# Two modulation blocks before the recurrence's first products, and 13 filler steps per pass in place of 14

## The reference, cut to what matters

```python
def step(S, inp):
    r_t, w_t, k_t, v_t, kk_t, a_t = inp
    sa = jnp.einsum('dbhvk,dbhk->dbhv', S, kk_t)
    S = (S * w_t[..., None, :] - sa[..., :, None] * (kk_t * a_t)[..., None, :]
         + v_t[..., :, None] * k_t[..., None, :])
    return S, jnp.einsum('dbhvk,dbhk->dbhv', S, r_t)
...
bonus = jnp.sum(jnp.sum(r * k * r_k, axis=-1, keepdims=True) * v, axis=0).reshape(B, L, C)
```

```python
s_lat = jax.nn.silu(c)[:, None, :]
s_ctx = jax.nn.silu(c_ctx)
for l in range(DEPTH):
    ml = jnp.split(s_lat @ w_mod[l] + b_mod[l], N_MOD, axis=-1)
    mc = jnp.split(s_ctx @ w_mod[l] + b_mod[l], N_MOD, axis=-1)
```

## Time and profile before

| | us |
|---|---|
| median of 3 runs | 3142.22 |
| lowest and highest of them | 3133.02, 3143.27 |
| the profiled execution | 3134.65 |
| its span (first to last instruction) | 3133.4 |
| PE busy in the span | 3004.9 |
| the four passes of the recurrence (first products of pass 0 to the last carried products) | 193.8 to 413.5 |

### The profile page before, as it was taken

How to read it: one execution, slowest core, us unless ns; L and a number is a source line. 1 busy time by engine, 2 the same in 40 slices (tenths; PEclk the granted TensorE clock), 3 DMA queues, 4 the chain that set the end, 5 groups by cost and what they waited for, 6 DMA issues and landing times.

```text
span 3133.4 us, 43817 instructions
## 1 busy us (share of the span) xinstructions
PE 3004.9 (96%) x18486; PEld 2429.1 (78%) x18486; DVE 1374.3 (44%) x2855; ACT 582.4 (19%) x1339; POOL 37.3 (1%) x60
## 2 busy tenths in 40 slices
PE   8988999999899999999999899999999999999999
PEld 7656778898488978888854447888878888765999
DVE  3264533433523544445222625445244453225675
ACT  1232222113412021100021621010010100124110
POOL 0000000002000000000000000000000000000000
PEclk9999999999999999999999999999999999999999
DMA  6667854366244452222212102222422222331453
GB/s 235 219 227 258 288 173 154 107 190 175 81 131 134 129 175 70 92 64 74 91 56 77 54 28 81 81 75 62 118 83 81 82 73 74 108 90 43 149 150 107
DMA packets 355846, 371.06 MB, mean 118 GB/s; under 512 B 7395, under 2 KB 282228, under 8 KB 355524
## 3 DMA queue, kind: packets, MB, share of 16 engines
q1 hardware_dynamic: 351828, 361.18, 36.5%
q0 software_dynamic: 2208, 5.31, 0.9%
q10 hardware_dynamic: 1616, 1.77, 0.2%
HBM read 367.19 MB, written 1.05 MB: 118 GB/s over the span
## 4 chain that ended last, share of the span: by engine, by line
PE 90%; DVE 5%; ACT 3%; issue 2%; DMA 0%; DVEq 0%; ACTq 0%
PE acc L132 74%; PE aux L132 15%; ACT sb_xn L275 1%; PE aux L2191 1%; DVE sb_work L1924 0%; DVE sb_work L1921 0%; ACT sb_work L1723 0%; ACT sb_work L1725 0%; DVE sb_xn L253 0%; ACT sb_rstd L266 0%; DVE sb_work L1935 0%; ACT sb_rstd L268 0%; DVE sb_work L1703 0%; DMA sb_x<-xT 0%; DVE sb_work L2341 0%
## 5 line engine op out<-in xcount | busy, mean ns | idle before, releaser
L132 PE MATMUL acc<-sb_xn,weights 128*128 128x256 f32 (+2 forms) x5184 | 1211.4, 388 | 16.2 <-DVE sb_xn L253 10.3
L132 PEld LDWEIGHTS acc<-sb_xn,weights 128*128 128x128 f32 x5184 | 942.2, 190 | 239.6 <-issue 118.8
L132 PE MATMUL acc<-sb_work 128*128 128x256 f32 (+1 forms) x1944 | 374.6, 346 | 0.0
L132 PEld LDWEIGHTS acc<-sb_work 128*128 128x128 f32 x1944 | 323.8, 191 | 34.7 <-issue 0.4
L132 PE MATMUL acc<-sb_work,weights 128*128 128x256 f32 (+2 forms) x1508 | 322.4, 361 | 3.2 <-DVE sb_work L1238 1.4
L132 PE MATMUL acc<-sb_big,weights 128*128 128x256 f32 (+1 forms) x1776 | 315.2, 334 | 4.1 <-issue 3.9
L132 PEld LDWEIGHTS acc<-sb_big,weights 128*128 128x128 f32 x1776 | 279.3, 192 | 30.8 <-issue 5.3
L132 PEld LDWEIGHTS acc<-sb_work,weights 128*128 128x128 f32 x1508 | 254.2, 191 | 54.3 <-issue 26.1
L1453 DVE TENSOR_TENSOR sb_work<-weights 128x512 f32<-128x512 f32 (+1 forms) x112 | 99.7, 890 | 160.6 <-PE acc L132 160.6
L1425 ACT COPY sb_work<-acc 128x256 f32<-128x256 f32 (+1 forms) x112 | 38.0, 339 | 704.7 <-PE acc L132 704.7
L132 PE MATMUL aux<-sb_xn,sb_work 128*128 128x256 f32 (+1 forms) x704 | 151.3, 359 | 8.9 <-ACT sb_xn L275 8.9
(11 more groups left out here) (305 smaller groups left out, 2591.8 us busy)
## 6 DMA issues: line engine op xcount, KB each, us to landing
weights<-ffn_w_up SPq DMA_DIRECT2D x88, 1024.0 KB, 7.9
weights<-w_mod SPq DMA_DIRECT2D x36, 2048.0 KB, 8.5
weights<-ffn_w_down SPq DMA_DIRECT2D x48, 1408.0 KB, 7.1
weights<-ffn_w_gate SPq DMA_DIRECT2D x44, 1024.0 KB, 5.4
weights<-w_in SPq DMA_DIRECT2D x8, 2048.0 KB, 8.0
weights<-mix_w_in SPq DMA_DIRECT2D x6, 2048.0 KB, 12.3
weights<-na_w_qkv SPq DMA_DIRECT2D x6, 2048.0 KB, 10.1
weights<-ple_w_gate SPq DMA_DIRECT2D x4, 2048.0 KB, 8.3
```

The lines of the kernel that those rows point to most:

```text
L132: return te.matmul(o, lhsT, rhs, start=start, stop=stop, skip_group_check=True)
```

## The change

The constant 20 takes the place of 16 as the base of `fill_at`, and 13 that of 14 as steps per pass. TensorE runs steps 17 to 20 (blocks 8 and 9, whole) after the bonus sum and before pass 0. VectorE runs its steps up to 18 at the end of the third part of its first preparation, ScalarE up to 18 after its first preparation. The total, 72 steps at the end of pass 3, is the same.

```diff
-    MOD_STEPS, MOD_EARLY = 36 * 2 + 1, 16
+    MOD_STEPS, MOD_EARLY, MOD_FIRST = 36 * 2 + 1, 16, 20
 
     def fill_at(p, point):
-        return min(MOD_STEPS, MOD_EARLY + 14 * p + point * 14 // 18)
+        return min(MOD_STEPS, MOD_FIRST + 13 * p + point * 13 // 18)
...
     def tensor_recurrence(other, first):
         for _ in first:
             pass
+        other.to(MOD_FIRST)
         for p in range(NP):
...
         for _ in first:
             pass
+        other.to(MOD_EARLY + 2)
         for p in range(NP):
             scalar_scan(p, other, scalar_prepare(p + 1) if p + 1 < NP else iter(()))
...
             if n == 1:
                 other.to(MOD_EARLY)
+            elif n == 2:
+                other.to(MOD_EARLY + 2)
```

## The result

The changed kernel takes 3142.35 us (median of 20 runs, 3138.62 to 3150.24). The kernel before was run 20 times as well: 3135.70 (3125.26 to 3143.27), so the three runs shown ahead of the prediction had given a high median. The ratio is 1.0020, with a 95% interval of 1.0013 to 1.0028: +6.6 us on the medians, where -6.0 had been forecast. The time lies inside the stated range, and by the 0.3% bound it is "same", but the direction was wrong. One execution of a later experiment (e10, 3533.16 us at a mean granted clock of 0.847) was in a slow state: the ratios leave it out, and without it e10's median is 3134.78 us instead of the 3135.16 of the table.

The account below looks back on a forecast made before the run. PE, busy 96% of the span, was taken as the bound, racing VectorE inside the levels. Pass sums of -2.5, -1.2, -2.4 and +0.1 made -6.0 us, from 3142.2 to 3136.2, range 3126 to 3145.

Parts of the forecast that it names:

- The four steps ahead of pass 0: Between bonus sum and pass 0: 5.08 us of steps fit PE's 6.8 us hole, cost nothing and leave 1.7 us.
- the new wait at point 2: Pass 0, point 2: PE waits 2.1 us for VectorE's bias addition, eating most of the 2.2 us clock gain.
- Rival 4: Before pass 0: the four steps run at half clock, pass 0 starts 2 us late; -2.7, 3139.5 us; chance 0.18.
- The levels: Inside the four passes: moved steps change the passes by -2.5, -1.2, -2.4 and +0.1 us, together -6.0.
- point 15: Late in each pass: its odd step is gone, giving -1.0 us per pass.
- the early odd steps: Odd steps at even points, partner just before, wait for VectorE: +1.8 us at point 10, +1.15 at point 14.
- the early odd step of point 18: End of passes 0 and 2: an odd step that must wait for VectorE's bias addition, about +0.15 us.
- What has no row of its own: Instruction-fetch stalls behind point 15 of passes 0, 1 and 3: taken as 0, bounds -3 and +3 us.
- Rival 2: In the passes: each early odd step's hole triggers half clock, 0.9 us each, nine times; +2.1, 3144.3 us; chance 0.12.
- Rival 3: In the passes: PE alone bounds, full clock gain and one fetch stall come back; -10.9, 3131.3 us; chance 0.20.
- the three signs that were to prove me wrong: Profile after: line 869 waits over 10 us, more stretches at 0.50 clock, or issue stalls over 3 from 8.3.

Follow-up runs that it names:

- run 20: Not a follow-up run: the words come from "was run 20 times", the kernel before, unchanged; median 3135.70 us (3125.26 to 3143.27).
- e10: Changed kernel plus 16 one-column matmuls in a start hole, shifting instruction pages a quarter page; 3135.16 us, ratio 0.9998 to the kernel before.
- e2: Changed kernel with 32 of 36 modulation weight loads cut to an eighth, modulation not computed; 3114.84 us, ratio 0.9940 to the kernel before.
- e1: Kernel before with 32 of 36 modulation weight loads cut to an eighth, modulation not computed; 3116.78 us, ratio 0.9946 to the kernel before.
- e9: Changed kernel plus 32 one-column matmuls in a start hole, shifting instruction pages half a page; 3118.19 us, ratio 0.9945 to the kernel before.
- e8: Kernel before with 13 steps per pass instead of 14, none ahead of pass 0, four left behind pass 3; 3130.43 us, ratio 0.9982.
- e7: Changed kernel with 14 steps per pass, VectorE also stopping at odd points and running steps 19 and 20 before pass 0; 3125.04 us, ratio 0.9965.
- e11: e7 plus 32 one-column matmuls in the start hole, a half-page shift; 3125.05 us, ratio 0.9971 to the kernel before.
- e12: e7 plus 48 one-column matmuls in the start hole, a three-quarter-page shift; 3126.42 us, ratio 0.9973 to the kernel before.

## Why the prediction was wrong, step by step

**The four steps ahead of pass 0** went as said: 1.9 us left of the hole (1.7 said), the weights were there, the first products at full clock and 1.98 us, and the new wait at point 2 took 2.06 (2.1 said). From the first products to level 1 pass 0 takes 9.55 us instead of 10.55: -1.0 for -1.1. Rival 4 did not happen.

**The levels.** With the loads cut, the differences between e2 and e1, worked out from the starts of each level's first product in their timelines, set beside the prediction:

| | start | level 1 | level 2 | level 3 | level 4 | level 5 | to point 16 | to the next pass | sum |
|---|---|---|---|---|---|---|---|---|---|
| pass 0 | -0.2 | +0.6 | -1.1 | +1.8 | -1.8 | +0.1 | -0.4 | +0.8 | -0.1 |
| forecast | -1.1 | +0.5 | -1.1 | +1.8 | -1.8 | +0.1 | -1.5 | +0.6 | -2.5 |
| pass 1 | -1.1 | +1.8 | -1.1 | +0.5 | -1.8 | +1.2 | -1.2 | 0.0 | -1.7 |
| forecast | -1.0 | +1.8 | -1.0 | +0.6 | -1.8 | +1.15 | -1.0 | 0 | -1.2 |
| pass 2 | -0.9 | +0.6 | -1.1 | +1.8 | -1.8 | +0.1 | -1.0 | +0.8 | -1.4 |
| forecast | -1.0 | +0.5 | -1.1 | +1.8 | -1.8 | +0.1 | -1.5 | +0.6 | -2.4 |
| pass 3 | -1.1 | +2.2 | -1.1 | +1.6 | -1.8 | +1.2 | -0.4 | +0.5 | +1.1 |
| forecast | -1.0 | +2.1 | -0.7 | +1.25 | -1.7 | +1.15 | -1.0 | 0 | +0.1 |

The forecast had -1.0 for point 15 and +0.1 for points 16 to 18 of passes 0 and 2; the rows divide the same total behind point 16, where an odd step stands in place of an even one (-0.5): -1.5 and +0.6.

Levels 1 to 5 of passes 0 to 2 came out within 0.1 us, the early odd steps among them. The sum is -2.1 instead of -6.0, for four reasons: e1 loses less at its start than the kernel before (half clock reaches 3.0 us into its pass 0 instead of 4.8; with real loads the term was -1.0); points 15 and 16 of passes 0 and 2 gave 0.5 less, and in pass 0 a page stall of 0.6 stands there; the early odd step of point 18 cost 0.2 more; and pass 3 was 1.0 short, all of it behind level 5. There e1 and e2 keep page stalls of 1.9 and 1.6 us (the last loads are of other weights and were not cut), and behind e2's the clock was at 0.50 for 3.4 us, behind e1's it was not: the next filler step took 1.94 us in e2 and 1.07 in e1. What covered the 0.5 at point 15 was not tried; the likely one is that PE now stands before the copies that the odd step had hidden.

**The step that failed** is "What has no row of its own": "I take 0, since three of four passes have the dense stretch at such a place either way". The mechanism was named rightly, and it was noted that the change moves the passes against the fetches' places. But the size was taken as one stall more or less, 3 us, by the count of passes, and put at 0. The measured change is +8.3 us of stalls (13 in place of 7), and behind them the clock was at half for 23.9 us in place of 10.2 (leaving out what followed the hole before pass 0). The stalls and half of the 13.7 us more at half clock come to some 15 us: as much as the whole difference between -6 and the stretch's +8.8. Two things were left undone. The stalls' places in the count of matmuls were a row each, and they are evenly spaced; with that, it could be read off which products of the changed program would stand at page ends, among them matmul 1992 right behind pass 0's densest products. And the half clock behind a stall was priced at 0.9 for each, from stalls of 2 to 2.6 us; behind 3.6 it lasted 6.8 us in pass 0 and 17 in pass 2.

**The rivals.** Rival 2 (slower, new holes throttle the clock) had the sign and the clock, but not the holes: those at the nine early odd steps were 0.74 to 2.06 us, and half clock stands behind the two fetch stalls of 3.5 to 3.7 us. That its 3144.3 lies 2 us from the measured time is luck. Rival 3 hoped for stalls that fall well; half a page of padding gave that, and more: e9's 3118 is below even its 3131. Of the three signs that were to prove me wrong one came: "stalls on issue differ from 8.3 by more than 3" (18.0). The waits for line 869 stayed under 10 us (9.3), and the stretches at half clock were fewer, two in place of four, though longer in sum.

**The base.** The median of three runs, 3142.2, was 6.5 us over that of 20. The forecast's 3136.2 was that median less 6, and so is near the kernel before as it was measured later. Against 3135.7 a forecast of -6.0 would have been 3129.7, and the measured 3142.35 lies 12.7 us over that: that it fell inside a range of 3126 to 3145 is luck, owed to the base and to the width of the range.

## What to carry to other kernels

Where TensorE is 96% busy on short products and a queue streams weights, list its waits without a releaser by their number in the program. If they are evenly spaced, as here at every 126.5 matmuls, they are likely instruction pages, and an edit that adds or moves instructions ahead of them shifts what stands there. One that is off the row can be something else, as e8's wait for weights was. Time such an edit at two or three paddings, of a quarter and half a page, before calling it good or bad: here the same change was worth +6.6 us at one and -10.1 (-8.5 by the ratios) at another. Fillers that feed one engine from another's stops should be placed so that the bank is freed a stop before it is wanted: a microsecond of such a wait cost a microsecond of the stretch here, and about half of one on the medians of the whole kernel.

## What the runs showed of the hardware

- An instruction page of 16 KB ends every 126.5 matmuls of the trace in this program. At its end TensorE waited up to 3.65 us for the next in the changed kernel, and up to 4.26 in e10, while 2 MB weight loads were in flight, and 0.6 us at the same product (1992) when the loads were an eighth (e2). In the stall that was looked at closely one packet of 16 KB from the instruction queue moved only once the weights' packets had thinned out (DMA share 1.00, then 0.20); in 63 of 64 stalls of over 1 us TensorE went on 1.2 to 1.6 us after such a packet had landed.
- TensorE's clock stood at 0.50, 1.2 GHz, behind the kernel before's stalls of 1.97 to 2.6 us for 3.4 us each, and behind the changed kernel's of 3.53 us for 17 us, with PE busy 13.9 of 16.7 us meanwhile. It stayed at 1.00 behind stalls of 3.35 us (e10) and 2.19 us (e7): the length of a stall alone did not decide it here.
- 128 idle instructions moved a kernel of 43817 by 24 us, 0.8%, and with 256 of them it was back.
- Why e11 and e12 keep the same median with stalls that differ by 3 us is open: runs of one kernel scatter over 3 to 18 us here, and each has one trace. Whether a fetch can be kept clear of a load, by smaller loads or by when they are issued, was not tried.
